# Padded row pitches for the four stationary operand tiles of a hybrid decoder block in split fp32

## The reference

```python
xn = rmsnorm(h, norm_w[l], NORM_EPS)
proj = xn @ w_in[l]                      # (256, 2048) @ (2048, 18432)
...
o_ret = rmsnorm(retention(rq, rk, rv), None, NORM_EPS) * silu(rz)
...
o_diff = rmsnorm(diff_attention(dq, dk, dv, lam), subln_w[l], SUBLN_EPS) * (1.0 - lam_init) * silu(dz)
mixed = (jax.nn.sigmoid(g_ret) * (o_ret @ w_ret_up[l])
         + jax.nn.sigmoid(g_diff) * (o_diff @ w_diff_up[l]))
h = h + mixed @ w_out[l]
return rmsnorm(h, final_norm_w, NORM_EPS)
```

## Time and profile before

| | us |
|---|---|
| median of 3 runs (lowest, highest) | 1128.18 (1128.13, 1130.06) |
| the profiled execution | 1128.63 |
| its span, first to last instruction | 1126.8 |
| TensorE busy, share of the span | 1114.4, 99% |
| TensorE weight loads, share | 924.1, 82% |
| VectorE busy, share | 613.7, 54% |
| ScalarE busy, share | 518.5, 46% |

### The profile page before, as it was taken

One profiled execution on the slowest core, in us unless ns is written; L12 is line 12 of the kernel. 1 busy time (PEld: TensorE's weight loads), 2 busy tenths in 40 slices (PEclk: granted clock), 3 DMA queues, 4 the chain that ended last, 5 costly groups with the idle time before them and its releaser, 6 DMA issues.

```text
span 1126.8 us, 13044 instructions
## 1 busy us (share of the span) xinstructions
PE 1114.4 (99%) x5038; PEld 924.1 (82%) x5038; DVE 613.7 (54%) x729; ACT 518.5 (46%) x672; POOL 47.8 (4%) x64
## 2 busy tenths in 40 slices
PE   8999999999999999999999999999999999999997
PEld 7888888888888888888888888888888888888885
DVE  6555454465545455455645565565656555566544
ACT  6544444443444443344553464446444554444443
POOL 0100000000000000000100001000100010000111
PEclk9999999999999999999999999999999999999999
DMA  9866656666655555666556656666666564555863
GB/s 345 265 182 204 181 162 188 190 185 178 191 171 168 188 196 194 188 189 185 169 168 189 188 167 179 186 178 175 178 185 187 168 190 168 188 187 185 291 200 108
DMA packets 108774, 213.54 MB, mean 190 GB/s; under 512 B 6692, under 2 KB 7976, under 8 KB 107944
## 3 DMA queue, kind: packets, MB, share of 16 engines
q1 hardware_dynamic: 107720, 209.02, 60.8%
q10 hardware_dynamic: 992, 3.68, 0.9%
HBM read 210.58 MB, written 2.10 MB: 189 GB/s over the span
## 4 chain that ended last, share of the span: by engine, by line
PE 98%; DMA 1%; issue 0%; DVE 0%; ACTq 0%; ACT 0%; POOLq 0%; POOL 0%; DVEq 0%
PE bank L903 31%; PE bank L905 31%; PE bank L904 31%; PE bank L912 1%; PE bank L922 1%; PE bank L929 1%; PE bank L1011 1%; PE bank L931 1%; PE bank L930 1%; DMA mixed<-x_t_dram 1%; PE bank L1015 0%; PE bank L1064 0%; PE bank L956 0%; PE bank L1023 0%; PE bank L957 0%
## 5 line engine op out<-in xcount | busy, mean ns | idle before, releaser
L607 DVE TENSOR_TENSOR w_lo<-raw,w_hi 128x1024 fp32r<-128x1024 f32 x383 | 475.1, 1241 | 478.1 <-ACT w_hi L402 477.1
L402 ACT ACTIVATE w_hi<-raw 128x1024 fp32r<-128x1024 f32 x383 | 405.9, 1060 | 574.3 <-PE bank L905 568.1
L903 PE MATMUL bank<-w_hi,xt_hi 128*128 128x512 f32 x1280 | 508.3, 397 | 2.4 <-DVE xt_lo L667 2.4
L905 PE MATMUL bank<-w_hi,xt_lo 128*128 128x512 f32 x1280 | 499.9, 391 | 0.0
L904 PE MATMUL bank<-w_lo,xt_hi 128*128 128x512 f32 x1280 | 498.9, 390 | 0.0
L905 PEld LDWEIGHTS bank<-w_hi,xt_lo 128*128 128x128 f32 x1280 | 240.6, 188 | 51.3
L903 PEld LDWEIGHTS bank<-w_hi,xt_hi 128*128 128x128 f32 x1280 | 240.9, 188 | 50.4 <-issue 2.7
L904 PEld LDWEIGHTS bank<-w_lo,xt_hi 128*128 128x128 f32 x1280 | 241.0, 188 | 48.4
L903 PE MATMUL bank<-w_hi,ot_hi 128*128 128x512 f32 x256 | 100.0, 391 | 0.0
L905 PE MATMUL bank<-w_hi,ot_lo 128*128 128x512 f32 x256 | 99.7, 389 | 0.0
L904 PE MATMUL bank<-w_lo,ot_hi 128*128 128x512 f32 x256 | 99.6, 389 | 0.0
(11 more groups left out here) (104 smaller groups left out, 392.2 us busy)
## 6 DMA issues: line engine op xcount, KB each, us to landing
raw<-w_in_dram SPq DMA_DIRECT2D x287, 512.0 KB, 3.8
raw<-w_ret_up_dram SPq DMA_DIRECT2D x32, 512.0 KB, 4.2
raw<-w_diff_up_dram SPq DMA_DIRECT2D x32, 512.0 KB, 3.7
raw<-w_out_dram SPq DMA_DIRECT2D x32, 512.0 KB, 4.2
gate<-x_dram SPq DMA_DIRECT2D x2, 1024.0 KB, 8.0
gate<-x_dram ACTq DMA_DIRECT2D x1, 2048.0 KB, 10.3
out_dram<-mixed SPq DMA_DIRECT2D x8, 256.0 KB, 2.7
mixed<-x_t_dram SPq DMA_DIRECT2D x2, 512.0 KB, 8.4
```

Of the source, the lines that this page charges most:

```text
L402: act.activation(w_hi[:, s, :, :], raw[:, s, :, :], ACT.Copy).then_inc(hi_ready, 1)
L607: dve.tensor_tensor(w_lo[:, s, :, :], raw[:, s, :, :], w_hi[:, s, :, :].bitcast(F32), ALU.subtract) \
L903: pe.matmul(bank[bk][:, :], hi, w_hi[:, s, kk, :], start=k == 0, stop=False)
L905: return pe.matmul(bank[bk][:, :], lo, w_hi[:, s, kk, :], start=False, stop=k == KT - 1)
```

## The change

Each of the four tiles is allocated with a longer row for each feature tile, and a slice hides the added words, so that every use of the tile stays as it is written. The row of `xt_hi` gets 257 words, that of `xt_lo` 264, that of `ot_hi` 258 and that of `ot_lo` 260, in place of 256. A load's 128 words stay adjacent; the byte at which feature tile k begins becomes 1028k, 1056k, 1032k and 1040k in place of 1024k.

```diff
-        xt_hi = sb("xt_hi", [P, KT, TOKENS], F32R)
-        xt_lo = sb("xt_lo", [P, KT, TOKENS], F32R)
-        ot_hi = sb("ot_hi", [P, KT, TOKENS], F32R)
-        ot_lo = sb("ot_lo", [P, KT, TOKENS], F32R)
+        xt_hi = sb("xt_hi", [P, KT, TOKENS + 1], F32R)[:, :, 0:TOKENS]
+        xt_lo = sb("xt_lo", [P, KT, TOKENS + 8], F32R)[:, :, 0:TOKENS]
+        ot_hi = sb("ot_hi", [P, KT, TOKENS + 2], F32R)[:, :, 0:TOKENS]
+        ot_lo = sb("ot_lo", [P, KT, TOKENS + 4], F32R)[:, :, 0:TOKENS]
```

## The result

| | before | after |
|---|---|---|
| median, us (runs) | 1128.60 (4) | 1150.21 (4) |
| lowest, highest | 1128.13, 1130.06 | 1149.04, 1151.14 |
| the profiled execution | 1128.63 | 1150.86 |
| its span | 1126.8 | 1149.1 |

The changed kernel is slower: the ratio is 1.0189, with a 95% interval of 1.0177 to 1.0201. The forecast was no change, 1128.5 us. The page after, answering to the earlier trace rows: TensorE's busy time grew by as much as the span, with the same instructions and the same clock.

The account below looks back on a forecast made before the run. The prediction took TensorE's 4608 large passes to bound the kernel. To the 1126.8 us span it added 0.3 for moved starts and zero for writers and later tiles: 1127.1 span, 1128.5 us forecast, 80% range 1106 to 1150.

Parts of the forecast that it names:

- What bounds the kernel: TensorE, busy 99% of the span; the 4608 passes at lines 903 to 905, 226.7 ns each, take 1044.6 us.
- an excess of 13.3 ns over 213.3: Each large pass takes 226.7 ns; 512 columns at 2.4 GHz need 213.3, leaving 13.3 ns, or 32 columns, on top.
- the price of the moved starts: Cost of new start addresses for the 4608 weight loads: put at 0.3 us, between 54 us less and 29 us more.
- rows 4 and 7: Earlier trace rows: equal pitch across passes, blocks and k, and 89 or 90 matmuls per 20 us on ot stretches.
- The prediction's own sign of being wrong: The pitch of the large passes moving by over half a nanosecond on average, 2.3 us over 4608 passes.
- Rival (a): Unaligned weight loads are served in two steps: in full 29.0 us more, 1157.2, milder forms 1130.5 to 1140; chance 32%.
- Rival (b): Load and stream conflict when low address bits agree; mixed offsets undo it: in full 54 us less, 1074; chance 22%.
- the two readers pass over each other's places: Argument against a conflict: a load reads 128 words in 0.11 us, the stream 512 in 0.21, wherever they begin.
- an estimate of 33 lines in place of 32: A 512-byte load beginning between two 16-byte lines touches one line more: a small addition, not a doubling.
- The writers and what lies behind: ScalarE and VectorE filling the four tiles in 80 instructions, and tiles allocated later moving 960 bytes: both put at nothing.
- The upper bound of the price: An unaligned load costs the excess twice: 2176 x 13.3 = 29 us more.
- rival (c): Load starts change but nothing in the read path looks at them: 1128.2 us; chance 46% together with the forecast.

Follow-up runs that it names:

- run 5: Kernel before with rows of 256 words, each pair of feature tiles shifted by its own 0 to 96 words, hi and lo equally, bases a multiple of 256 bytes from streams: 1149.30 us.
- run 6: As run 5, at 16 other shifts: xt units 5 to 15 words, ot units 20 to 112 words, no unit unshifted: 1153.18 us.
- run 7: As run 5, but hi tiles unshifted and only the lo tiles shifted unit by unit: 1145.71 us.
- run 8: Kernel before with only the streamed tile w_lo beginning 64 bytes later, all loads as before: 1149.53 us.
- run 9: Kernel before with a 64-byte tile ahead of raw, so streams and loads all move together: 1128.23 us.
- run 1: Kernel before with only the lo tiles padded, xt_lo to 264 and ot_lo to 260 words: 1147.31 us, ratio 1.0169.
- run 3: Kernel before with all starts on 16 bytes or better: rows of 264 words in both xt tiles, 260 in both ot tiles: 1153.58 us.
- run 11: Kernel before with only a pad of 240 words in front of mixed, moving all later tiles by 960 bytes: 1129.37 us.
- run 2: Kernel before with only the hi tiles padded, xt_hi to 257 and ot_hi to 258 words, which also moves the lo tiles: 1149.73 us, ratio 1.019.
- run 10: Kernel before with w_hi, w_lo and the four tiles all beginning 4 bytes later, distances kept at multiples of 256 bytes: 1174.79 us.

## Why the prediction was wrong, point by point

**What bounds the kernel** was right: the passes at lines 903 to 905, read from start to start, carry the difference (20.2 of 22.3 us behind the first group), and an excess of 13.3 ns over 213.3 was the thing to ask about. What the change adds on top comes from the two readers of SBUF: the pitch answers to the distance between their addresses (runs 5 to 9), and at 427 ns it doesn't change. That the 13.3 ns themselves come from them isn't shown, since no run took them away.

**The step that failed** is the price of the moved starts: "Between ends so far apart I go by rows 4 and 7, which say that offsets do nothing". They said it of steps of 512 and 1024 bytes. The pattern repeats every 256, so each of those steps returned to the same distance, and the trace of before held only one. An even pitch at multiples of the period isn't evidence for the places between. The term taken as 0.3 us measured 4608 x 4.5 ns = 20.7 us, by a mechanism that isn't in the sum: a distance to the stream, which slows the aligned loads as well. The prediction's own sign of being wrong, a pitch that moves by over half a nanosecond on average, came true: it moved by 4.5, on unaligned and aligned loads alike.

**Rival (a)** had the sign and, in full, the order of magnitude, but not the mechanism. It expected 2176 slow loads and fast ones at k = 0, 4, 8, 12, xt_lo and ot_lo; instead the passes of all lines are slow alike, the means on xt lie between 230.0 and 233.2 ns for every k, k = 0, 4, 8 and 12 too, and run 1 loses 18.7 us without one load off 16 bytes.

**Rival (b)** had the place: addresses of load and stream against each other. Its sign was wrong, because it took the fixed distance of before as a collision to be undone. That distance, a multiple of 256 bytes, is one of the three best of 31. The hint that was read against the change's loss, the pitch wandering to 0.24 behind small matmuls, shows much the same range (223 to 240 before) that the changed kernel lives in all the time; I took it as a sign that something could be gained.

**The 13.3 ns themselves** stayed: no distance tried has a mean below 226.7. My argument that the two readers pass over each other's places wherever they begin is right in that the excess doesn't vanish, and wrong in that it stays equal.

**The Trainium skill's rules.** The Trainium skill's 16-byte lines (Advanced Engine Details and Errata, SBUF Cachelines) gave the prediction an estimate of 33 lines in place of 32, a small loss that depends on k. Runs 1 and 3 lose 18.7 and 25.0 us without a load off 16 bytes, so the loss isn't this. The Trainium skill's rule that a load takes no read bandwidth from the matmul that runs beside it (TensorE: Matmul & The Clock Gate, Step-by-step: what each phase is for) doesn't fit what was measured: run 8 against run 9 is 64 bytes between the two readers, and 21.3 us.

**The writers and what lies behind** were rightly put at nothing: the writers' means are within 3 ns of those before, and run 11 is at 1129.37, within the 1.5 us expected.

**The range** ended at 1150, where the result fell: the four runs' median of 1150.21 is a fifth of a microsecond beyond it, the ratio times the 1128.18 that the forecast was built on, 1149.5, just inside. Either way that is luck. The upper bound of the price came from an unaligned load costing the excess twice on 2176 loads; the true loss was a third of the excess, on all passes. The stretch from 1135 to 1150 had been given 11%, all of it to rival (a), which is not what happened.

**A slip without effect:** the sum gives 1128.5 us, and rival (c), called the same forecast, 1128.2.

**Open:** why 240 bytes is good while 16 isn't, and why in run 1, where only lo is apart, the ot passes of k = 1 and k = 9 (lo 16 and 144 bytes off) still go at 226 or 227 ns; why one load in three off the distance spoils nearly all (run 7: 16.9 us); why pitches at a constant distance alternate or repeat by threes; where the 13.3 ns come from; and what an aligned load beside an unaligned stream would do. No run was made for these.

## What to carry to other kernels

Where float32r passes of 128x512 with a fresh weight load each run back to back at full clock, keep the start of the stationary and of the moving operand at one distance, a multiple of 256 bytes, with both on 16 bytes, and count the tiles allocated ahead; rows of one and two words more in the hi tiles, which also push the lo tiles by 64 and 192 bytes, cost 1.9% (run 2), and 4 bytes on all operands 4% (run 10). Read the pitch from starts: the recorded duration of one pass (397 ns before, 402 after) isn't the time that it takes in the sequence. And before "addresses don't matter" is concluded from a trace, ask which addresses the trace contains: all may be multiples of the period in question.

## What the runs showed of the hardware that was not expected

- The pitch of a 128x512 float32r pass with its own load settles at 226.7 ns at distances of 0, 240 and 256 bytes between load and stream, and has means of 228.5 to 234.5 at the 28 others tried.
- Consecutive passes aren't independent: with one stream in three off, all three passes scatter (224 to 241 ns in run 8), and after a return to a good distance it takes three matmuls until they are even again (run 6: 238, 232, 229, then 227).
- At one constant distance the pitch can alternate (236 and 231 ns at 64 bytes) or repeat by threes (231, 238, 231 at 160 bytes), in runs 5 and 6.
- With stream and loads both 4 bytes off and a good distance, the pitch is even at 237.8 ns.
- At the pace of 1.2 GHz the padded kernel has 426 ns, as the kernel before, and so has run 6 with all its loads moved.
